# One encoder layer on one core: where the expert weights live, and in which order the first expert pairs, the router and the last rows are worked on

## The chip, the core and the metric

The kernel runs on one core of a Trainium2 chip. The metric is device time in microseconds (us) of one execution. Five engines work side by side, each through its own list of instructions: TensorE (PE, with its weight loads as PEld), VectorE (DVE), ScalarE (ACT), GpSimd (POOL) and SyncE (SP). SyncE issues every large DMA of this kernel, in one order, and waits on semaphores between them.

## The reference, cut to what matters

Input x is (1, 256, 1024) float32. One layer is computed:

```
proj  = x @ w_in                                  # 1024 -> 6144
conv  = pointwise(swish(LN(depthwise31(GLU(proj)))))
attn  = windowed attention (8 heads, band 128) @ w_attn
mixed = (sigmoid gate * conv + sigmoid gate * attn) @ w_out
x1    = LN(alpha * x + mixed; ln1)
top group of 4, then top 2 of its 8 experts per token, with weights
moe   = sum over 32 experts of weight * (silu(x1 @ gate_e) * (x1 @ up_e)) @ down_e
out   = LN(alpha * x1 + moe; ln2)
```

Each token goes to 2 of 32 experts. An expert's gate and up weights are 1024 x 512 floats, 2.10 MB; its down weights are 256 x 1024 floats, 1.05 MB.

## The kernel before, in words

**Projection stages (0 to 233 us).** The dense products run over 72 weight blocks (48 of w_in, 8 each of attention, convolution and output projection). SyncE loads block b into one of four `raw` buffers once GpSimd has split block b-4. ScalarE casts a block to a high part (L611), GpSimd computes the low part (L540), TensorE multiplies with three products (L1334 to L1336). Between the blocks SyncE already loads some expert weights.

**Homes of expert weights.** `slots` has four places, each for one expert's gate/up and down weights. `extra`, `spare` and `late` hold one expert's gate/up weights each. A home of gate/up weights has two halves with a semaphore each. Experts 0, 1 and 4 and the down weights of 0 and 1 are loaded among the blocks of w_in. Slots 2 and 3 lie over `over`, a region that holds the convolution and attention arrays (`h_pad`, `acc`, `qT`, `v_sb`, `prob`, `dist`), so experts 2 and 3 are loaded after the last block has been issued. Expert 5 goes to `spare` once the output projection is done. From expert 6 on there are seven gate/up homes in rotation and four down homes; down weights of pair p are loaded when pair p-2's down products are done (`down_done` of 2(p-1) in SyncE's loop), and gate/up weights run a few experts ahead (`refilled_to`).

**Residual and router (233 to 242 us).** ScalarE copies the four banks of the residual sum to `xt` (`copy_r`). TensorE transposes them (`turn_r`) into banks 0, 1, 2 and again 0; ScalarE copies the parts of token tile 0 and VectorE those of tile 1 to `x1T`. VectorE gathers the moments (`moments`), ScalarE the deviation. ScalarE normalizes from the banks (`normalize_rows`) and casts. TensorE computes logits (L1504, L1512), VectorE picks the experts, TensorE the ranks (L1534 to L1539).

**Pairs.** Experts are worked on two at a time, 64 token places each: 16 pairs. For a pair p: GpSimd copies its tokens from the sorted `xgT` (L569); TensorE makes gate/up products into bank 0 (`gate_up`, L1592); ScalarE applies silu (`swish`, L787); VectorE multiplies with up and weight (`gate_times_up`, L1219); TensorE turns h (`turn_h`, L1616); ScalarE copies it (`copy_hT`, L793); TensorE makes the down products into banks 1 and 2 (`down`, L1627); ScalarE casts y's high part (`split_y_hi`, L800), VectorE subtracts (`split_y_lo`, L1233); TensorE scatters high and low part into banks 3 to 6 (`scatter`, L1642 and L1643). A look-up (`slot_info`, L1576) gives the token and weight of each place; `copy_info` (L776, L779) copies it. VectorE builds the matrices of scatter and look-up (L1226, L1189, L1194). TensorE's order for pair p is: gate/up of p, scatter of p-1 (first half), turn of p, scatter of p-1 (second half), look-up of p+1, down of p.

**First pairs.** Tokens of pairs 0 and 1 are gathered by a product of their own (`gather_first`, L1550 and L1552). Pair 0 runs first. All tokens are then sorted by `gather_sorted` (L1566, L1567) behind the gate/up products of pair 1, through banks 3 to 6, and copied to `xgT`, which lies in `gates` (L806, L1240). GpSimd meanwhile applies gain and offset of the first LayerNorm to `xt` (L558, L561).

**Tail.** After the last scatter VectorE takes the moments of four half rows (L1087), ScalarE the deviation (L726). Half (0,0) is scaled by ScalarE (L852) and finished by GpSimd (L592, L594); the other three by VectorE with two instructions each (L1306, L1307). SyncE stores each half.

## Time and profile before

| what | us |
|---|---|
| median of 3 runs | 475.8 (475.67 to 477.68) |
| the profiled execution's own time | 475.59 |
| its span in the profile | 473.8 |
| TensorE busy | 458.0 (97%) |
| VectorE, ScalarE, GpSimd busy | 248.9, 206.7, 223.1 |
| moved by DMA | 145.13 MB, mean 306 GB/s |

A busy share is a mean over stages with different limits. The slices of the page give it by time; the chain of waits names for each moment the instruction that the end of the span hangs on; a timeline gives the instructions of an engine in order. In a chain of waits "issue" is time in which an engine waited for nothing that the profile shows. Each native float32 product counts as two records of TensorE.

### The profile page before, as it was taken

How to read it: one execution, taken by the hardware profiler on the slowest of the kernel's cores; microseconds unless marked ns; L12 is line 12 of the kernel's file. 1: busy time of each engine (PE TensorE's matmuls, PEld its weight loads, DVE VectorE, ACT ScalarE, POOL GpSimd, SP SyncE). 2: the span in 40 equal slices, each digit the busy share in tenths (PEclk: the TensorE clock that was granted, in tenths of full speed). 3: DMA queues.
4: the chain of work that ended last, by engine and by line, in shares of the span. 5: the costliest groups of instructions: out<-in, count | busy, mean ns of one | idle time of the engine just before them, and what ended most of it. 6: DMA issues, size and time to landing. Idle time of an engine off the chain costs nothing.

```text
span 473.8 us, 7652 instructions
## 1 busy us (share of the span) xinstructions
PE 458.0 (97%) x2776; PEld 321.6 (68%) x2776; DVE 248.9 (53%) x547; ACT 206.7 (44%) x463; POOL 223.1 (47%) x190
## 2 busy tenths in 40 slices
PE   8999999999999999999988999999999999999991
PEld 7999999889999999998863644444444334444430
DVE  3089999869998565466387332222222122222116
ACT  4544455478885678445683232221121122222212
POOL 3998989946956679999448021111111001111002
PEclk9999999999999999999999999999999999999996
DMA  8899989534433444556998999999999999999912
GB/s 282 297 377 361 362 293 356 200 117 144 158 130 121 135 139 174 189 176 245 428 380 326 422 396 423 423 422 419 422 419 422 420 423 420 421 420 423 420 55 91
DMA packets 27091, 145.13 MB, mean 306 GB/s; under 512 B 3120, under 2 KB 3376, under 8 KB 14512
## 3 DMA queue, kind: packets, MB, share of 16 engines
q1 hardware_dynamic: 27056, 144.65, 77.7%
q8 instruction: 23, 0.38, 0.3%
q14 instruction: 12, 0.10, 0.1%
HBM read 143.59 MB, written 1.05 MB: 305 GB/s over the span
## 4 chain that ended last, share of the span: by engine, by line
PE 94%; DVE 3%; ACT 2%; issue 1%; POOL 0%; DVEq 0%; ACTq 0%; POOLq 0%
PE bank L1592 23%; PE bank L1334 14%; PE bank L1336 13%; PE bank L1335 13%; PE bank L1627 12%; PE bank L1642 4%; PE bank L1643 3%; PE bank L1414 1%; PE bank L1392 1%; PE bank L1362 1%; PE bank L1616 1%; PE bank L1566 1%; PE bank L1567 1%; PE bank L1402 1%; PE bank L1421 1%
## 5 line engine op out<-in xcount | busy, mean ns | idle before, releaser
L540 POOL TENSOR_TENSOR w_lo<-raw,w_hi 128x512 fp32r<-128x512 f32 x140 | 182.8, 1323 | 43.8 <-ACT w_hi L611 40.2
L611 ACT CAST w_hi<-raw 128x512 fp32r<-128x512 f32 x140 | 85.4, 620 | 76.7 <-PE bank L1336 73.8
L1334 PE MATMUL bank<-x_hi,w_hi 128*128 128x256 f32 x400 | 115.5, 289 | 0.0
L1336 PE MATMUL bank<-x_hi,w_lo 128*128 128x256 f32 x400 | 113.4, 283 | 0.0
L1335 PE MATMUL bank<-x_lo,w_hi 128*128 128x256 f32 x400 | 113.3, 283 | 0.0
L883 DVE SCALAR_TENSOR_TENSOR bank<-slots,par,bank 128x256 f32<-128x256 f32 x232 | 92.4, 484 | 0.3
L569 POOL COPY raw<-gates 128x512 f32 x28 | 19.8, 708 | 151.1 <-PE bank L1592 134.6
L1592 PE MATMUL bank<-slots,raw 128*64 128x512 f32 x320 | 84.5, 593 | 0.0
L1334 PEld LDWEIGHTS bank<-x_hi,w_hi 128*128 128x128 f32 x400 | 76.8, 192 | 0.6 <-POOL w_lo L540 0.2
L1335 PEld LDWEIGHTS bank<-x_lo,w_hi 128*128 128x128 f32 x400 | 76.8, 192 | 0.3
L1336 PEld LDWEIGHTS bank<-x_hi,w_lo 128*128 128x128 f32 x400 | 76.8, 192 | 0.0
L1627 PE MATMUL bank<-slots,kT 128*64 128x512 f32 x256 | 58.5, 599 | 0.4 <-ACT kT L793 0.4
L1592 PEld LDWEIGHTS bank<-slots,raw 128*64 128x64 f32 x320 | 27.6, 137 | 44.6 <-issue 44.6
L1219 DVE SCALAR_TENSOR_TENSOR pT<-pT,kT,bank 128x256 f32<-128x256 f32 x16 | 7.7, 481 | 91.5 <-ACT pT L787 91.5
L1233 DVE TENSOR_TENSOR w_lo<-bank,w_hi 128x512 fp32r<-128x512 f32 x32 | 22.0, 690 | 56.9 <-ACT w_hi L800 56.9
L787 ACT ACTIVATE pT<-bank 128x256 f32<-128x256 f32 x16 | 6.2, 385 | 97.0 <-PE bank L1592 97.0
L1627 PEld LDWEIGHTS bank<-slots,kT 128*64 128x64 f32 x256 | 17.2, 137 | 28.3 <-issue 28.1
L800 ACT CAST w_hi<-bank 128x512 fp32r<-128x512 f32 x32 | 18.7, 585 | 36.8 <-PE bank L1627 36.8
L1642 PE MATMUL bank<-w_hi,w_lo 128*128 128x512 f32 x64 | 28.3, 441 | 1.2 <-DVE gates L1240 0.9
L1592 PE MATMUL bank<-spare,raw 128*64 128x512 f32 x64 | 28.1, 593 | 0.0
L1592 PE MATMUL bank<-extra,raw 128*64 128x512 f32 x64 | 28.1, 593 | 0.0
L1592 PE MATMUL bank<-late,raw 128*64 128x512 f32 x64 | 28.1, 593 | 0.0
(224 smaller groups left out, 648.8 us busy)
## 6 DMA issues: line engine op xcount, KB each, us to landing
slots<-in_w_gate_up SPq DMA_DIRECT2D x40, 1024.0 KB, 13.3
slots<-in_w_down SPq DMA_DIRECT2D x32, 1024.0 KB, 13.2
raw<-in_w_in SPq DMA_DIRECT2D x45, 512.0 KB, 3.7
extra<-in_w_gate_up SPq DMA_DIRECT2D x8, 1024.0 KB, 12.5
spare<-in_w_gate_up SPq DMA_DIRECT2D x8, 1024.0 KB, 16.4
late<-in_w_gate_up SPq DMA_DIRECT2D x8, 1024.0 KB, 15.8
raw<-in_w_attn SPq DMA_DIRECT2D x8, 512.0 KB, 3.3
raw<-in_w_conv SPq DMA_DIRECT2D x8, 512.0 KB, 3.3
```

Of the source, the lines that this page charges most:

```text
L540: nc.gpsimd.tensor_tensor(w_lo[:, n % SPLIT, m], raw[:, raw_of(b), m], w_hi[:, n % SPLIT, m].bitcast(F32), ALU.subtract).then_inc(w_lo_don ...
L569: ins = nc.gpsimd.tensor_copy(xg[u][:, :, j * WIN:(j + 1) * WIN], xgT[:, :, bass.ds(at, WIN)])
L611: nc.scalar.copy(w_hi[:, n % SPLIT, m], raw[:, raw_of(b), m]).then_inc(w_hi_done, 1)
L800: nc.scalar.copy(y_hi[:, c * HALF:(c + 1) * HALF], y_bank[c][:]).then_inc(y_hi_done, 1)
L883: ins = nc.vector.scalar_tensor_tensor(dst, h_pad[:, i, tap:tap + SEQ], w, so_far, ALU.mult, ALU.add)
L1233: nc.vector.tensor_tensor(y_lo[:, n], y_bank[c][:], y_hi[:, n].bitcast(F32), ALU.subtract).then_inc(y_lo_done, 1)
L1334: mm(dst, ah, bh, start=first, stop=False, **kw)
L1335: mm(dst, ah, bl, start=False, stop=False, **kw)
L1336: return mm(dst, al, bh, start=False, stop=last, **kw)
L1592: ins = mm(gu_bank[j * WIN:(j + 1) * WIN, :], xg[u][:, k, j * WIN:(j + 1) * WIN], weights(j, k // (KT // 2), k % (KT // 2) == 0)[:, n], st ...
L1627: ins = mm(y_bank[c][j * WIN:(j + 1) * WIN, :], hT[:, k, j * WIN:(j + 1) * WIN], w[:, k, c * HALF:(c + 1) * HALF], start=(k == 0), stop=(k ...
L1642: mm(dst, s, y_hi[:, n], start=False, stop=False, skip_group_check=True)
```

## The change

Five edits, made together:

1. **Homes.** Gate/up weights have three homes for pairs (slots 0 and 1; slots 2 and 3; `extra` and `spare`), in rotation. Down weights have a ring of three pairs too (two halves of `late`; slots 0 and 1; slots 2 and 3), and pair 0's lie in `gates`. Pair p is refilled when pair p-3 has read its weights.
2. **Loads.** Experts 2 and 3 and the down weights 4 and 5 are issued between the blocks 61 to 71, as soon as `over` is free; down weights 0 and 1 after the last block; ln1's rows go to `raw`, ln2's rows to slot 2 near the end.
3. **Order of the first pairs** on TensorE: gate/up 0, look-ups 0 and 1, gate/up 1 (into bank 6, with h of pair 0 turned in its middle), down 0, turn 1, `gather_sorted`, look-up 2, down 1, both halves of scatter 0, then pair 2. ScalarE and VectorE follow; their loops over pairs are written out.
4. **Router.** The fourth transpose goes to bank 3; ScalarE copies three of four parts; VectorE copies its part ahead of the last moments; rows are normalized from `xt`; seven products instead of three keep TensorE busy.
5. **Tail.** The second half of the last scatter uses y in float32 (`y_last`) instead of a high and a low part. Token tile 1 is finished as ((r - mean) * gain + std * offset) / std: VectorE the first part, TensorE adds std * offset by a product with a diagonal matrix, ScalarE scales.

```diff
-WARM_START, WARM_ROUTE, WARM_PLACE = 3, 3, 1
+WARM_START, WARM_ROUTE, WARM_PLACE = 3, 7, 1
+RING = 3
+def gu_home_of(e):
+    return (e % 2, 2 + e % 2, EXTRA + e % 2)[e // 2 % RING]
+def wd_home_of(e):
+    if e < 2:
+        return FIRST + e
+    return (LATE + e % 2, e % 2, 2 + e % 2)[e // 2 % RING]
...
@@ SyncE
                 if b == 18:
-                    load_down(0)
-                    load_down(1)
+                    load_down(2)
+                    load_down(3)
...
+                if b == OVER_FREE:                       # OVER_FREE = 61
+                    sp.wait_ge(silu_done, KT)
+                    sp.wait_ge(c_lo_done, KT)
+                    sp.wait_ge(pv_done, HEADS)
+                if OVER_FREE <= b < OVER_FREE + 8 and (b - OVER_FREE) % 2 == 0:
+                    load_half(2 + (b - OVER_FREE) // 4, (b - OVER_FREE) // 2 % 2)
+                if b == OVER_FREE + 8 or b == OVER_FREE + 10:
+                    load_down(4 + (b - OVER_FREE - 8) // 2)
             sp.wait_ge(m_lo_done, KT // 2)
+            load_down(0)
+            load_down(1)
+            sp.wait_ge(w_lo_done, 2 * splits_before(N_BLOCKS))
             sp.dma_start(ln_rows, ln1.broadcast_to([P, 2, D])).then_inc(s_ln1, 16)
-            sp.wait_ge(silu_done, KT)
-            sp.wait_ge(pv_done, HEADS)
-            for e in (2, 3):
-                load_gate_up(e)
-            for e in (2, 3):
-                load_down(e)
...
+            def refill(p):
+                for c in range(2):
+                    sp.wait_ge(gu_done if c else gu_half_done, p - RING + 1)
+                    for e in (2 * p, 2 * p + 1):
                         load_half(e, c)
+            def refill_down(p):
+                sp.wait_ge(down_done, 2 * (p - RING + 1))
+                for e in (2 * p, 2 * p + 1):
                     load_down(e)
+            refill(RING)
+            refill(RING + 1)
+            sp.wait_ge(gathered, KT)
+            refill_down(RING)
+            refill_down(RING + 1)
+            for p in range(RING + 2, PAIRS):
+                refill(p)
+                refill_down(p)
+            sp.wait_ge(gu_done, PAIRS - 2)
+            sp.dma_start(ln2_rows, ln2.broadcast_to([P, 2, D])).then_inc(s_ln2, 16)
...
@@ ScalarE
-            copy_rT(0, 0)
+            copy_rT(0, 0, 0)
             deviation(0)
+            copy_rT(2, 0, 1)
+            copy_rT(3, 1, 1)
             deviation(1)
-            copy_rT(2, 1)
...
+            swish(0)
             copy_info(0, 0)
+            act.wait_ge(info_copied, 1)
+            copy_info(1, 1)
+            copy_hT(0)
+            swish(1)
+            split_y_hi(0)
+            copy_hT(1)
+            copy_sorted()
+            copy_info(2, 0)
+            split_y_hi(1)
+            for p in range(2, PAIRS):
+                pair(p, p % 2)
...
             deviation(0, TT)
+            deviation(1, TT)
+            act.wait_ge(ln_std, 2 * TT)
+            nc.scalar.mul(std_diagonal, ident, mv[:, 1, 2:3]).then_inc(std_turned, 1)
             act.wait_ge(last_shift, 1)
             nc.scalar.activation(xt[:, 0, 0:HALF], out_bank[0][:], ACT.Identity, scale=mv[:, 0, 3:4],
                                  bias=mv[:, 0, 4:5]).then_inc(last_z, 1)
-            deviation(1, TT)
+            for c in range(2):
+                act.wait_ge(offset_added, c + 1)
+                nc.scalar.mul(xt[:, 1, c * HALF:(c + 1) * HALF], out_bank[2 + c][:],
+                              mv[:, 1, 3:4]).then_inc(result_by_act, 1)
...
@@ VectorE
+            for p in range(2):
+                gate_times_up(p, p)
+                build_scatter(p, p)
+                build_gather(p + 2, p)
+            split_y_lo(0)
+            copy_sorted()
+            split_y_lo(1)
...
             inverse(0, TT)
             shift(0, last_shift)
-            last_normal(0, 1)
             inverse(1, TT)
-            last_normal(1, 0)
-            last_normal(1, 1)
+            for c in range(2):
+                r = out_bank[2 + c][:]
+                nc.vector.scalar_tensor_tensor(r, r, mv[:, 1, 0:1], ln2_rows[:, 0, c * HALF:(c + 1) * HALF],
+                                               ALU.subtract, ALU.mult).then_inc(centred_rows, 1)
+            # then half (0, 1), its two instructions as before
...
@@ TensorE
             gather_first()
+            gate_up(0, 0)
             slot_info(0, 0)
-            gate_up(0, 0)
-            for p in range(PAIRS):
+            pe.wait_ge(compact_built, 1)
+            slot_info(1, 1)
+            gate_up(1, 1)                    # turns h of pair 0 after its first half
+            down_pair(0)
+            turn_h(1)
+            gather_sorted()
+            slot_info(2, 0)
+            down_pair(1)
+            pe.wait_ge(xgT_odd, KT // 2)
+            pe.wait_ge(xgT_even, KT // 2)
+            for c in range(2):
+                scatter(0, 0, c)
+            for p in range(2, PAIRS):
                 pair(p)
...
+            for c in range(2):
+                pe.wait_ge(centred_rows, c + 1)
+                mm(out_bank[2 + c][:], std_diagonal, ln2_rows[:, 1, c * HALF:(c + 1) * HALF], start=False, stop=True,
+                   skip_group_check=True).then_inc(offset_added, 1)
```

## Rows read from the trace of the kernel before

**Rows 1.** the page's slices (40 of equal length) and its row of the block splits

```profile
GB/s 282 297 377 361 362 293 356 200 117 144 158 130 121 135 139 174 189 176 245 428 380 326 422 396 423 423 422 419 422 419 422 420 423 420 421 420 423 420 55 91
...
L540 POOL TENSOR_TENSOR w_lo<-raw,w_hi 128x512 fp32r<-128x512 f32 x140 | 182.8, 1323 | 43.8 <-ACT w_hi L611 40.2
```

**Rows 2.** chain of waits, 0 to 464 us; columns: start, length (us), what ran

```profile
246.36 7.04 PE bank L1592 x32
...
255.42 3.66 PE bank L1627 x16
...
259.08 6.87 PE bank L1592 x32
...
273.49 0.82 DVE gates L1240
...
274.35 0.50 PE bank L1642
...
280.40 6.87 PE bank L1592 x32
...
288.39 0.31 PE bank L1616 x2
...
448.62 6.87 PE bank L1592 x32
```

**Rows 3.** timeline of TensorE, look-up; columns: start, length (us), engine, line, operation

```profile
276.54 0.28 PE L1576 MATMUL bank<-info,gat 128*128 128x6 f32 x2
```

**Rows 4.** timelines of ScalarE and TensorE in the router

```profile
235.66 0.78 ACT L742 ACTIVATE xt<-bank,mv 128x512 f32<-128x512 f32 x1
...
240.91 0.27 PE L1534 MATMUL bank<-onehot,sums 128*128 128x64 f32 x1 [1.79 <-DVE onehot L1154]
```

**Rows 5.** timelines of VectorE and GpSimd around the first pairs

```profile
255.67 2.57 DVE L1189 TENSOR_TENSOR gat<-con,rt 128x256 fp32r<-128x256 f32 x1
...
258.16 2.38 DVE L1194 CAST info<-weights 128x4 fp32r<-128x4 f32 x2
...
255.56 4.89 POOL L561 TENSOR_TENSOR xt<-xt,gates 128x1024 f32<-128x1024 f32 x2
...
275.61 2.87 POOL L569 COPY raw<-gates 128x512 f32 x4 [14.57 <-issue]
```

**Rows 6.** timeline of SyncE's queue, DMA issues

```profile
176.46 20.69 SPq L444 DMA_DIRECT2D raw<-in_w_conv  x8
...
220.95 2.74 SPq L419 DMA_DIRECT2D slots<-in_w_gate_up  x4
```

**Rows 7.** windows; columns: busy us of PE, PEld, DVE, ACT, POOL, clock, DMA share, GB/s

```profile
210.00:220.00 10.00, 10.00 (x51) 8.43 (x50) 7.95 (x11) 5.18 (x9) 9.84 (x9) 1.00 0.58 196
...
246.40:250.00 3.60, 3.60 (x18) 1.24 (x20) 3.39 (x13) 3.57 (x7) 0.00 (x0) 1.00 0.40 162
...
452.00:454.00 2.00, 2.00 (x12) 0.60 (x10) 0.00 (x0) 0.00 (x0) 0.00 (x0) 1.00 0.11 45
```

**Rows 8.** DMA issues of 199 to 221 us: count, KB each, median us to landing

```profile
raw<-in_w_out SPq DMA_DIRECT2D x8, 512.0 KB, 4.2
```

**Rows 9.** block casts on ScalarE (L611), 30 to 70 us: idle before them

```profile
  DMA raw<-in_w_in: 2.5, 2
```

**Rows 10.** timelines of ScalarE and GpSimd in the tail

```profile
461.49 0.59 ACT L800 CAST w_hi<-bank 128x512 fp32r<-128x512 f32 x1 [1.13 <-PE bank L1627]
...
467.43 1.26 POOL L592 TENSOR_TENSOR xt<-xt,raw 128x512 f32<-128x512 f32 x1 [35.46 <-ACT xt L852]
```

**Rows 11.** chain of waits, ends of the span

```profile
5.57 6.91 PE bank L1362 x32
...
463.24 1.91 DVE stat L1087 x3
...
470.27 0.75 DVE xt L1307
```

**Rows 12.** window in the tail, columns as in rows 7

```profile
466.00:467.00 1.00, 0.00 (x0) 0.00 (x0) 0.96 (x4) 0.50 (x1) 0.00 (x0) 0.50 0.00 0
```

More of the change, by code:

```diff
@@ L811, in copy_sorted, with pair @@
                         nc.scalar.mul(out_bank[k % 4][:], xt[:, k % 4 // 2, 0:HALF], ALPHA).then_inc(sums_by_act, 1)
[L813 removed]
+            def pair(p, u):
                 swish(p)
[L815 to L816 removed]
                 copy_hT(p)
[L818 removed]
+                if p < PAIRS - 1:
                     copy_info(p + 1, 1 - u)
@@ L1229, in split_y_lo @@
             def split_y_lo(p):
-                for c in range(2):
+                for c in range(1 if is_pair(p, PAIRS - 1) else 2):
                     n = slice(c * HALF, (c + 1) * HALF)
@@ L1286, in _ @@
             for p in range(2):
-                pair(p, p)
-            with dve.Fori(1, PAIRS // 2 - 1) as i:
-                for u in range(2):
-                    pair(i * 2 + u, u)
-            for p in range(PAIRS - 2, PAIRS):
-                pair(p, p % 2, build=False)
-            load = dve.value_load(load_i[0:1, 0:1], min_val=0, max_val=SEQ)
+                gate_times_up(p, p)
[5 more added lines that the diff above has]
+            for p in range(2, PAIRS):
+                if p == PAIRS - 1:
+                    load = dve.value_load(load_i[0:1, 0:1], min_val=0, max_val=SEQ)
+                pair(p, p % 2)
             with dve.If(load > WIN):
@@ L1636, in scatter @@
                     pe.wait_ge(sums_by_dve if c else sums_by_act, TT)
-                pe.wait_ge(y_lo_done, 2 * p + (c + 1))
+                whole = is_pair(p, PAIRS - 1) and c == 1
+                if whole:
+                    pe.wait_ge(y_hi_done, 2 * PAIRS)
+                else:
+                    pe.wait_ge(y_lo_done, 2 * p + (c + 1 - unsplit(p)))
                 for t in range(TT):
@@ L1641, in scatter @@
                     n = slice(c * HALF, (c + 1) * HALF)
+                    if whole:
+                        ins = mm(dst, s.bitcast(F32), y_last, start=False, stop=True, skip_group_check=True)
+                        ins.then_inc(scattered if t == TT - 1 else last_done, 1)
+                        continue
                     mm(dst, s, y_hi[:, n], start=False, stop=False, skip_group_check=True)
```

205 lines of the change are left out of this document (95 added, 110 removed).

## The prediction

> **What bounds the kernel now.** I read the page's slices first, then the chain of waits, then the timelines of each engine where the chain leaves TensorE, and last SyncE's queue and the DMA windows. TensorE is busy for 97% of the span, so only three things can move the end: a gap of TensorE closed, work taken out of the tail that follows it, or a new gap opened. In the slices the reader sees something else as well: from slice 20 on DMA moves about 420 GB/s almost without a break [rows 1]. One pair needs two times 2.10 and two times 1.05 MB, 6.29 MB or 14.95 us at 420.7 GB/s (the middle of those slices), while TensorE needs a pair every 12.94 us: the gate/up products begin at 280.40 for pair 2 and at 448.62 for pair 15, thirteen periods [rows 2]. So loads lose 2.0 us to TensorE with each pair and live on their lead. In the window from 452 on only 45 GB/s are left [rows 7]: the stream ends near 452. Its last piece are two down loads (2.1 MB, 5.0 us), so the last gate/up half lands near 447, and pair 15 begins at 448.62. The lead at the end is a mere 2 us for the first half. An earlier TensorE alone would have run into the loads.
>
> The chain leaves TensorE at three places that the change touches. Gate/up of pair 0 ends at 253.40 and its down products start at 255.42; of these 2.02 us the turn takes 0.31 and the look-up about 0.2 (the 0.28 of its row overlaps the next product's start at about 276.74), so 1.5 are a wait for silu, multiply and copy [rows 2, 3]. After the sort TensorE waits from 273.49 to 274.35, 0.86 us, for VectorE's copy [rows 2]. And behind the last scatter a chain on VectorE runs from 463.24 to 470.27 + 0.75 = 471.02 [rows 11].
>
> **The first pairs.** Every product of before is in the new order too; what goes are the two waits, 1.5 + 0.86 = 2.4 us. Which waits could take their place? I put the new order on a time line. The look-up no longer stands before gate/up 0, which may start 0.2 us earlier, and costs its 0.2 behind it. Gate/up 0 ends near 253.1, the look-ups 0 and 1 at 253.5. ScalarE does silu (0.39) and then two copies of look-ups (0.8 each, by their rows of before), VectorE multiplies by 255.0; the turn in the middle of gate/up 1 comes at 257.0 and finds it done, 2 us to spare. Gate/up 1 ends at 260.7, down 0 at 264.3. Silu and multiply of pair 1 must be ready by then. Here VectorE is slow: beside GpSimd's LayerNorm operations its builds take 2.57 and 2.38 us [rows 5], and they stand ahead of the multiply of pair 1. They end with GpSimd's, near 261, so the multiply ends near 261.9, 2.4 us before the turn needs it. The sort runs 264.6 to 272.1, waits for GpSimd's x1 near 261 (its last pair of operations ends at 260.45 now [rows 5], some 0.5 later then). Look-up and down 1 (3.6) now cover VectorE's last copy. Scatter 0 takes 2.0, and gate/up 2 begins at 277.95 instead of 280.40. It needs GpSimd's token copies: before they began 1.3 us after the last copy at 274.30 and pair 2's two of the four take half of 2.87 [rows 5]; on the new line that is 272.9 + 1.3 + 1.4 = 275.6, in time. I take 2.5 us, with 0.5 and 2.8 as ends: the low end is a copy or build on ScalarE or VectorE that comes 2 us late. The period of 12.94 stays: same products, no wait inside it.
>
> **The router.** TensorE's own work up to the logits stays, so the fourth bank and the other division of copies save at most the 0.3 us that the last copy may hold up. Against that, VectorE's moments of tile 1 now stand behind a copy (0.68), so the shift of tile 0 and with it ScalarE's first normalized row move from 235.66 to about 236.1 [rows 4]. Four rounds of 1.33 end then at 240.9 to 241.0, about where TensorE makes the ranks at 240.91 [rows 4], and it waits for them. Cost 0.1 (0.0 to 0.4). The four extra products (256 columns in float32, 0.43 each: 6.91 us for 16 [rows 11]) lie in its 1.79 us of idle [rows 4] and end at 240.7, just in time; without that cover they would cost up to 1.7.
>
> **Loads.** By the issues of the convolution blocks (8 in 20.69 us, one each 2.9 [rows 6]) block 61 is issued near 190.9. From there six loads of 1.05 MB stand between blocks that leave 42% of DMA time free [rows 7]: 6.3 MB, 15 us of DMA that before began at 220.95 [rows 6]. The region is free by then: VectorE's last low part of the convolution, its last reader, ends at 186.4 in its timeline. On the other side the new homes leave DMA idle from about 239 (expert 5 landed) to 249.8 (first half of gate/up 0 done), where before it idled only in part [rows 7], and again from 270 to 272, as the down loads of pair 3 wait for the sort. From 272.2 on it never stops: 26 down and 22 gate/up loads, 73.4 MB, 174.5 us, end 446.7; the last gate/up half lands 5 us before, at 441.7, and is wanted at 448.62 - 2.5 + 3.4 = 449.5, its first half (436.7) at 446.1. The lead at the end is 8 to 9 us instead of 2. So loads bind nowhere, and the gain of the first pairs reaches the end. ln2's rows follow by 449, wanted at 464.
>
> What the early loads cost the blocks: one now lands 4.2 us after issue [rows 8]. A block's turn on GpSimd comes after three others, 6 x 1.32 = 7.9 us [rows 1], its cast on ScalarE up to 1.5 before that: 6.4 us are allowed. A load ahead of it adds at most 1.05 MB, 2.5 us less what drains before, say 0.9: 5.1. Cost 0; the high end is that of the block casts near 30 us, where whole experts go out at once: 2.5 us in two waits [rows 9], 1.25 for each of six loads, 7.5 us.
>
> **The tail.** Down 15 ends as before; I keep its clock, 461.47. The second scatter half now is two native products of 0.86 (twice the 0.43 for 256 columns [rows 11]) where four of 0.23 stood, but it starts behind the first half at 462.3 and not at 462.85, behind ScalarE's cast (461.49 + 0.59 [rows 10]) alone; TensorE ends at 464.05 in both. What gains is VectorE: without the subtraction the moments begin near 462.0 instead of 463.24 [rows 11] and end near 464.9 instead of 465.94. The shift of tile 0 comes near 465.4, 1.0 earlier, the deviation of tile 1 at 465.5. VectorE then has four instructions of 0.75 instead of six: centred rows at 466.5 and 467.2, half (0,1) at 468.7. GpSimd's two of 1.26 [rows 10] begin at 466.7 and end at 469.3. TensorE adds the offsets at 466.5: 0.86 each at full clock, ScalarE's last scaling ends at 469.1, and with the stores in a row behind GpSimd's the last is issued at 469.8, against 471.05: 1.2 us gained. At half clock each product takes 1.73, the last scaling ends at 470.7 and the gain is 0.3. Now the clock was 0.50 at 466 to 467 [rows 12], TensorE having been idle from 464.05. I take 0.7, between the two, since the moment of the fall need not be the same; the ends are -0.3 (a product waits for both) and 1.3.
> The Trainium skill speaks against this edit: "TensorE: Matmul & The Clock Gate", Part 1 on the clock gate, has TensorE at 1.2 GHz once it was idle and at 2.4 only after sustained work. By that rule, if the fall has come first, the tail gains 0.3; by a clock that still holds, 1.2. The trace agrees that the clock falls after the last scatter.
>
> **The sum.** 2.5 - 0.1 + 0 + 0.7 = 3.1 us off a span of 473.8: 470.7, or 472.5 of the profiled execution's own 475.59 (1.8 lie outside the span). The median of the runs is 0.2 higher, 475.8, and gives 472.7.
>
> **The rivals.**
> 1. *The early loads delay the blocks.* For it: DMA would be 90% full from 191 to 220, GpSimd has no slack there (9.84 of 10 us [rows 7]), so each late block moves the end. Against: the margin of 1.3 us. It decides when a block takes longer than 6.4 us to land. At its full price, 475.8 + 7.5 - 3.1 = 480.2; above 5.5 us of delay the kernel is slower than before by more than 0.5%. Chance 0.07.
> 2. *A new wait takes the place of those removed in the first pairs:* VectorE's builds, slowed by GpSimd, hold the multiply of pair 1, or the copies of the sort hold GpSimd's tokens for pair 2. For it: the long builds of rows 5. Against: margins of 2.4 and 2.3 us. It leaves 0.5 of the 2.5 us: 474.7. Chance 0.15.
> 3. *The change doesn't do what it says in the tail:* TensorE's clock is down and its products, with two more hand-overs, end no earlier than VectorE did alone. For it: rows 12. Gain of the tail 0 to -0.3: 473.4 to 473.7. It is part of my own range at its slow end; chance that it holds alone 0.12 (around the bound of 0.5%).
> 4. *The loads bind,* as the rotation of homes leaves DMA idle for 11 us that I have wrong by some us more, or ScalarE's and VectorE's longer written-out code is fetched late through the full queues. For it: 2 us lost per pair. Against: the lead of 8 us, and TensorE's own code, written out before, which shows no such wait. It would cost 3 to 6 us: 476 to 479. Chance 0.06.
> My forecast, 472.7 with its own range of 471.4 to 473.7, has 0.60.
>
> **How the numbers follow.** A measurement of this kernel tells about 0.5% from no change, 2.4 us: faster means below 473.4. Of my forecast's 0.60, 0.58 is faster; rival 3 adds 0.05 and rival 2 0.01: 0.64. Within 0.5%: 0.02 of mine, 0.07 of rival 3, 0.14 of rival 2 and 0.04 of rivals 1 and 4 (a small price of theirs that eats the gain): 0.27. Slower: the 0.09 that is left of rivals 1 and 4. The range takes in my own terms with their bounds and rival 2: 471.0 (0.4 below the sum of good ends, for what the router may give) to 475.2.
>
> **What would show it.** In the changed profile: gate/up products of pairs 0 and 1 back to back but for two look-ups and a turn; no gap above 0.3 us on TensorE up to gate/up 2, which begins near 278; a period of 12.94 to the end; the early loads' blocks landing in about 5 us and no wait of ScalarE's casts for DMA after 190; DMA silent between about 239 and 250 and done before 450; the first moments of the tail 1.2 us after the last down product's first half was scattered. I am wrong if gate/up 0 begins later than 247, if ScalarE waits for raw blocks, or if gate/up products of a late pair wait for a load. The clock at the two offset products decides the last us.

## The result, and the profile after

The changed kernel takes 473.33 us (median of 5 runs, 473.14 to 473.68), the one before 475.8; the ratio is 0.9942 (95% interval 0.9922 to 0.9962). The profiled execution took 473.26 with a span of 471.5, against 475.59 and 473.8. Forecast were 472.7 and a range of 471.0 to 475.2: the sign and the range hold, and 3.1 us were forecast where 2.3 (spans) to 2.5 (medians) came. The kernel before varies more than this: one of its five runs here took 477.68, and more such runs follow under warm_route.

The slices of the page after (11.8 us each): against [rows 1] GB/s rise in slices 17 to 19 (189 to 224 us), where the early loads now run, and fall in slice 20; slice 21 is a hole.

```profile
GB/s 292 291 378 360 343 301 359 198 120 140 164 133 135 136 134 177 295 358 341 340 187 281 423 325 419 422 423 420 422 420 422 421 422 420 420 420 423 423 116 91
```

The chain of waits after, from the first gate/up products on (start, length in us, what ran):

```profile
246.26 7.02 PE bank L1638 x32
253.28 0.54 PE bank L1622 x4
253.81 3.58 PE bank L1638 x16
257.40 0.37 PE bank L1664 x2
257.77 3.58 PE bank L1638 x16
261.35 3.43 PE bank L1676 x16
264.78 0.37 PE bank L1664 x2
...
272.56 3.58 PE bank L1676 x16
...
278.18 7.02 PE bank L1638 x32
...
446.54 6.87 PE bank L1638 x32
```

These answer to the chain of [rows 2]. The two gaps of before are gone: gate/up 0 ends at 253.28 and gate/up 1 starts at 253.81 behind two look-ups, the turn of pair 0 sits in its middle (257.40), down 0 follows at 261.35 and the sort at 265.15. Pair 2 begins at 278.18 and not at 280.40, pair 15 at 446.54 and not at 448.62. VectorE and GpSimd at the places that the forecast named as risks:

```profile
256.11 2.57 DVE L1233 TENSOR_TENSOR gat<-con,rt 128x256 fp32r<-128x256 f32 x1
258.60 2.40 DVE L1238 CAST info<-weights 128x4 fp32r<-128x4 f32 x2
261.82 0.48 DVE L1263 SCALAR_TENSOR_TENSOR pT<-pT,kT,bank 128x256 f32<-128x256 f32 x1 [0.82 <-ACT pT L824]
```

```profile
274.60 2.88 POOL L605 COPY raw<-gates 128x512 f32 x4 [9.22 <-issue]
```

The builds take 2.57 and 2.40 as in [rows 5]. They end at 261.00, and VectorE then stands idle for 0.82 us until silu of pair 1 is done, so they hold nothing up. The multiply starts at 261.82 and its turn comes at 264.78. GpSimd's copies start at 274.60; pair 2's are done 2.1 us before they are wanted.

DMA after, in windows (busy us of PE, PEld, DVE, ACT, POOL, clock, DMA share, GB/s), beside [rows 7]:

```profile
210.00:220.00 10.00, 10.00 (x51) 8.48 (x50) 7.82 (x12) 5.16 (x9) 9.84 (x8) 1.00 0.96 363
240.00:250.00 10.00, 9.69 (x60) 6.29 (x60) 7.81 (x38) 8.50 (x17) 2.68 (x3) 1.00 0.13 54
270.00:275.00 5.00, 5.00 (x25) 2.98 (x25) 3.01 (x4) 3.12 (x9) 0.40 (x1) 1.00 0.54 190
450.00:454.00 4.00, 4.00 (x19) 1.44 (x16) 0.13 (x1) 0.39 (x1) 0.00 (x0) 1.00 0.33 137
```

The last loads of gate/up weights, in SyncE's queue and by their time to landing (count, KB each, us):

```profile
411.19 9.79 SPq L448 DMA_DIRECT2D slots<-in_w_gate_up  x4
```

```profile
slots<-in_w_gate_up SPq DMA_DIRECT2D x1, 1024.0 KB, 26.4
```

The stream of weights has the forecast hole from 240 and a smaller one at 270, and ends at about 450 + 4 x 137 / 421 = 451.3. The last gate/up half, issued at 420.6, lands at 447.0 (26.4 us later); pair 15 wants it at 450.0. The tail:

```profile
460.07 2.03 DVE L1136 BATCH_NORM_STATS2 stat<-bank 128x6 f32<-128x512 f32 x3 [1.07 <-PE bank L1700]
...
464.67 2.96 PE L1761 MATMUL bank<-slots,sig 128*128 128x512 f32 x4 [2.45 <-DVE bank L1364]
...
465.96 0.69 ACT L902 ACTIVATE xt<-bank,mv 128x512 f32<-128x512 f32 x1 [1.33 <-PE bank L1761]
...
466.67 2.04 SPq L548 DMA_DIRECT2D out_x<-xt  x4
467.66 0.69 ACT L902 ACTIVATE xt<-bank,mv 128x512 f32<-128x512 f32 x1 [1.02 <-PE bank L1761]
```

```profile
464.00:465.00 1.00, 0.33 (x1) 0.30 (x2) 1.00 (x2) 0.63 (x1) 0.22 (x1) 1.00 0.00 0
465.00:466.00 1.00, 1.00 (x3) 0.47 (x2) 0.96 (x3) 0.04 (x1) 1.00 (x1) 0.74 0.00 0
466.00:467.00 1.00, 1.00 (x2) 0.05 (x1) 0.63 (x1) 0.65 (x1) 0.92 (x2) 0.50 0.00 0
```

TensorE's clock falls at about 465.5 (0.74 is the mean of 465 to 466), within the first of the two offset products. TensorE had been idle from 462.2 to 464.67. The second product, the last two of the four records, runs wholly at the low clock.

The start of an execution varies: gate/up 0 began between 246.13 and 247.07 us in profiled executions of kernels that are the same up to there (the changed kernel, old_tail, old_rows, warm_tail, warm_stores). The earliest and the latest of all kernels, homes_swap and then warm_tail, with TensorE's first native products and ScalarE's first residual copy:

```profile
5.09 7.07 PE L1394 MATMUL bank<-gates 128*128 128x256 f32 x32
...
230.74 2.63 ACT L754 COPY xt<-bank 128x512 f32<-128x512 f32 x4 [1.26 <-PE bank L1368]
```

```profile
5.74 7.66 PE L1407 MATMUL bank<-gates 128*128 128x256 f32 x32
...
231.98 2.63 ACT L767 COPY xt<-bank 128x512 f32<-128x512 f32 x4 [1.26 <-PE bank L1381]
```

The products end at 12.16 and 13.40, 1.24 us apart, and the copies are 1.24 apart too: the whole difference arises in the first 13 us. What varies is how fast TensorE runs at first. Its opening products, small ones that only keep it busy, have weight loads of 0.34 us and later of 0.19 us. The tail of the changed kernel has the same two lengths, 0.34 at a granted clock of 0.50 and 0.19 at 1.00:

```profile
465.71 0.34 PEld L1761 LDWEIGHTS bank<-slots,sig 128*128 128x128 f32 x1 [0.29 <-issue]
```

In homes_swap the short ones begin before the products above, in warm_tail only within them, between 6.6 and 7.0 us. By these lengths TensorE starts at the low level and rises sooner or later; the clock row itself reads 1.00 there, so it can't confirm this. In thirteen of the fourteen profiled executions of the table below it takes 218.56 to 218.59 us from the end of these products to the residual copy. The changed kernel's took 218.89. It had lost 0.3 us by 98 us; before that one of ScalarE's casts waited 3.1 us for its block, where no other execution has a wait above 2.5. The early loads come later than that, and six of the thirteen have them: they cost the projection stages nothing.

So I compare stages, from the profiled execution of each kernel. "Residual copy" is the start of ScalarE's first copy of the residual sum, "gate/up 0 to 2" goes from the start of pair 0's gate/up products to the start of pair 2's, "cast" is the start of ScalarE's copy of the last half of y, "first moments" are VectorE's first in the tail. All in us:

| kernel | median | residual copy to gate/up 0 | gate/up 0 to 2 | gate/up 2 to 15 | cast to first moments | cast to last result | cast to end of span |
|---|---|---|---|---|---|---|---|
| before | 475.8 | 15.32 | 34.04 | 168.22 | 1.75 | 9.53 | 12.31 |
| changed | 473.33 | 15.08 | 31.92 | 168.36 | 0.66 | 8.94 | 12.09 |
| late_loads | 473.29 | 15.09 | 31.92 | 168.37 | 0.66 | 7.99 | 11.94 |
| old_order | 476.59 | 15.20 | 34.02 | 168.22 | 0.66 | 9.64 | 12.82 |
| old_homes | 478.77 | 15.08 | 31.93 | 173.02 | 0.64 | 9.21 | 12.34 |
| homes_swap | 473.35 | 15.08 | 31.92 | 168.51 | 0.65 | 8.87 | 11.99 |
| old_router | 473.45 | 15.19 | 31.93 | 168.36 | 0.64 | 7.96 | 11.89 |
| hoist_only | 475.58 | 15.33 | 34.02 | 168.22 | 1.22 | 8.99 | 11.81 |
| old_tail | 473.25 | 15.08 | 31.93 | 168.37 | 1.22 | 8.99 | 11.60 |
| old_rows | 472.47 | 15.08 | 31.93 | 168.35 | 0.66 | 8.62 | 11.28 |
| warm_tail | 473.92 | 15.09 | 31.92 | 168.37 | 0.66 | 8.00 | 11.87 |
| warm_stores | 473.37 | 15.08 | 31.92 | 168.37 | 0.66 | 8.00 | 11.97 |
| simple | 473.34 | 15.08 | 31.92 | 168.37 | 0.67 | 8.63 | 11.48 |
| warm_route | 476.08 | 15.31 | 34.04 | 168.21 | 1.76 | 9.53 | 12.39 |

From gate/up 15 to the cast it is 12.87 everywhere. The columns repeat to within 0.03 where two kernels have the same code there, so a stage tells 0.1 us where a median does not tell 0.5. The last two columns are excepted, since the clock and the stores come in: the end of the span differs by 0.2 between kernels with the same tail (hoist_only and old_tail, old_rows and simple). The change's 2.3 us are +0.14 up to the residual copy, then -0.24, -2.12, +0.14 and -0.22 up to the end of the span. Nearly all of it lies between gate/up 0 and 2, where the order of the first pairs was changed.

### The profile page after: what moved, and what is told of

The parts are those of the page before. It is cut to its first block, busy times and chain, and to the rows that moved or that the text cites. A ratio compares the mean times of both kernels' runs of the same rounds, so it can differ in the third digit from the quotient of the medians.

```text
span 471.5 us, 7554 instructions
## 1 busy us (share of the span) xinstructions
PE 463.3 (98%) x2788; PEld 323.0 (69%) x2788; DVE 244.2 (52%) x543; ACT 208.9 (44%) x467; POOL 223.2 (47%) x190
## 4 chain that ended last, share of the span: by engine, by line
PE 94%; ACT 3%; DVE 1%; issue 1%; POOL 0%; ACTq 0%; DVEq 0%; POOLq 0%
PE bank L1638 23%; PE bank L1379 14%; PE bank L1381 13%; PE bank L1380 13%; PE bank L1676 12%; PE bank L1699 4%; PE bank L1700 3%; PE bank L1459 1%; PE bank L1437 1%; PE bank L1407 1%; PE bank L1664 1%; DVE stat L1136 1%; PE bank L1613 1%; PE bank L1612 1%; PE bank L1447 1%
## 5 line engine op out<-in xcount | busy, mean ns | idle before, releaser
L1638 PE MATMUL bank<-slots,raw 128*64 128x512 f32 x352 | 77.7, 593 | 0.0
L1638 PEld LDWEIGHTS bank<-slots,raw 128*64 128x64 f32 x352 | 25.0, 137 | 48.9 <-issue 48.7
L1676 PE MATMUL bank<-slots,kT 128*64 128x512 f32 x160 | 36.5, 598 | 0.0
L1638 PE MATMUL bank<-extra,raw 128*64 128x512 f32 x80 | 35.2, 593 | 0.0
L1638 PE MATMUL bank<-spare,raw 128*64 128x512 f32 x80 | 35.2, 593 | 0.0
L1699 PE MATMUL bank<-w_hi,w_lo 128*128 128x512 f32 x62 | 27.3, 440 | 0.0
L1638 PEld LDWEIGHTS bank<-extra,raw 128*64 128x64 f32 x80 | 10.9, 137 | 22.6 <-issue 22.6
L1700 PE MATMUL bank<-w_lo 128*128 128x512 f32 x62 | 24.5, 396 | 0.0
```

Source lines behind the costliest of these rows:

```text
L1638: ins = mm(gu_bank(p)[j * WIN:(j + 1) * WIN, :], xg[u][:, k, j * WIN:(j + 1) * WIN], weights(j, k // (KT // 2), k % (KT // 2) == 0)[:, n], ...
L1676: ins = mm(y_bank[c][j * WIN:(j + 1) * WIN, :], hT[:, k, j * WIN:(j + 1) * WIN], by_row(weights(j))[:, k, n], start=(k == 0), stop=(k == H ...
L1699: mm(dst, s, y_hi[:, n], start=False, stop=False, skip_group_check=True)
L1700: ins = mm(dst, s, y_lo[:, n], start=False, stop=True, skip_group_check=True)
```

## The experiments

**late_loads: the early loads undone.**

```diff
-                if b == OVER_FREE:
...
-                if OVER_FREE <= b < OVER_FREE + 8 and (b - OVER_FREE) % 2 == 0:
-                    load_half(2 + (b - OVER_FREE) // 4, (b - OVER_FREE) // 2 % 2)
-                if b == OVER_FREE + 8 or b == OVER_FREE + 10:
-                    load_down(4 + (b - OVER_FREE - 8) // 2)
...
+            for e in (2, 3):
+                load_gate_up(e)
...
             load_down(0)
             load_down(1)
+            for e in (4, 5):
+                load_down(e)
```

> The changed kernel with one thing undone: gate/up weights 2 and 3 and down weights 4 and 5 are issued behind the last block (after 220 us) and no longer between blocks 61 and 71. Theory A, the early loads only fill time that is free later: in the changed kernel DMA stands idle from 240 to 249.9 (0.13 busy), and six loads of 2.5 us moved there leave it idle from about 248 only. Then nothing moves: 473.3 us within 0.3, gate/up 2 at 278.2, the stream of weights ends at 451.3 as now, blocks land in 4.2 us again. Theory B, the early loads give the stream its lead: the stream ends 10 us or more later, gate/up products of the last pairs wait for their weights, 476 to 480 us.

473.29 us, ratio to before 0.9931 (0.9909 to 0.9952), and no stage up to the first moments changed. (The last result came 0.95 us earlier since the clock had not fallen in this execution; see the tail below.) Its windows:

```profile
210.00:220.00 10.00, 10.00 (x53) 8.50 (x52) 7.49 (x11) 4.82 (x9) 9.85 (x8) 1.00 0.55 187
240.00:250.00 10.00, 9.69 (x59) 6.43 (x60) 7.75 (x40) 8.51 (x16) 3.01 (x3) 1.00 1.01 417
450.00:454.00 4.00, 4.00 (x19) 1.30 (x16) 0.00 (x0) 0.20 (x1) 0.00 (x0) 1.00 0.47 195
```

The loads fill 240 to 250, where the changed kernel had 54 GB/s, and the stream ends at 450 + 4 x 195 / 421 = 451.9, against 451.3 in the changed kernel; 0.3 of that is its later start. Theory A: the early loads only move the hole.

**old_order: the first pairs in the order of before.**

```diff
-            gate_up(0, 0)
-            slot_info(0, 0)
-            slot_info(1, 1)
-            gate_up(1, 1)
-            down_pair(0)
-            turn_h(1)
-            gather_sorted()
...
+            slot_info(0, 0)
+            gate_up(0, 0)
+            turn_h(0)
+            slot_info(1, 1)
+            down_pair(0)
+            gate_up(1, 1)
+            gather_sorted()
+            scatter(0, 0, 0)
+            turn_h(1)
+            scatter(0, 0, 1)
...
```

> The changed kernel with the order of the first two pairs put back on TensorE, ScalarE and VectorE (turn and down of pair 0 directly behind its gate/up, the sort behind gate/up 1, all gate/up products in bank 0); homes, loads, router and tail stay. Theory A, the order brought the gain up to pair 2: gate/up 2 begins at 280.3 instead of 278.18, the period stays 12.94, 475.4 us. Theory B, homes and loads brought it: gate/up 2 stays near 278.2 and the time at 473.3.

476.59 us, ratio 0.999 (0.9974 to 1.0005). The chain:

```profile
247.07 7.04 PE bank L1636 x32
...
281.09 6.87 PE bank L1636 x32
```

34.02 us from gate/up 0 to 2, as before: the order is worth 2.10 to 2.12 us (theory A). The median lies 1.2 above the expectation. Its 12 runs fall in two groups, four at 474.8 to 475.3 with a mean clock of 0.999 to 1.000, which is what was expected, and eight at 476.4 to 476.9 with 0.995 to 0.996. The profiled execution (476.73) is of the second group. It started 0.8 us later than the changed kernel's, and it took 9.64 us to the last result: both offset products ran at the low clock, four records in 3.65 us where the changed kernel had 2.96. No execution of the first group was profiled.

```profile
467.44 3.65 PE L1757 MATMUL bank<-slots,sig 128*128 128x512 f32 x4 [2.45 <-DVE bank L1363]
```

**old_homes: homes, refills and row places of before under the new order.**

```diff
-EXTRA, GU_HOMES = SLOTS, SLOTS + 2
+SPARE, TOKENS, EXTRA = SLOTS, SLOTS + 1, SLOTS + 2
+HOMES = SLOTS + 3
...
-            refill(RING)
-            refill(RING + 1)
...
+            refill((6, 7))
+            for p in range(SLOTS // 2, PAIRS):
+                sp.wait_ge(down_done, 2 * (p - 1))
+                for e in (2 * p, 2 * p + 1):
+                    load_down(e)
+                if p == SLOTS // 2:
+                    refill((8, 9))
+                refill(range(refilled_to(p - 1), refilled_to(p)))
```

> The changed kernel with the homes, the refills and the places of the LayerNorm rows of before (seven gate/up and four down homes, nothing of experts 2 and 3 before the last block); order of the pairs, router and tail stay changed. Theory A, an earlier TensorE alone runs into the loads: before, the last gate/up halves landed about 446 and 448 where pair 15 began at 448.6; now it begins at 446.5, so TensorE waits up to 1 us in the late pairs: 473.5 to 474.4 us. Theory B, the stream moves with TensorE, as its refills are released by it, and nothing binds: 473.3. Theory C, the gain is that of the homes: 475 or more.

478.77 us, ratio 1.0045 (1.0028 to 1.0062): slower than before, and by far more than theory A had. Theory C's number (475 or more) came, and its reason is refuted by the next run. TensorE waits for down weights of pairs 7 and 8. The rows say "issue", but the second load of each pair, issued at 330.8 and 343.7, lands 22.5 and 24.5 us later, at 353.3 and 368.2, just as the products begin:

```profile
353.39 3.65 PE L1664 MATMUL bank<-slots,kT 128*64 128x512 f32 x16 [0.71 <-issue]
...
368.30 3.65 PE L1664 MATMUL bank<-slots,kT 128*64 128x512 f32 x16 [1.91 <-issue]
```

and once more in pair 14 (1.37 us ahead of its down products and 0.5 inside its gate/up products). SyncE's queue shows where the lead went:

```profile
250.18 4.25 SPq L442 DMA_DIRECT2D slots<-in_w_gate_up  x4
265.12 0.81 SPq L451 DMA_DIRECT2D slots<-in_w_down  x2
265.97 2.21 SPq L442 DMA_DIRECT2D slots<-in_w_gate_up  x4
```

```profile
260.00:270.00 10.00, 10.00 (x47) 5.62 (x44) 5.52 (x11) 3.39 (x6) 1.72 (x2) 1.00 0.55 214
```

In the new order down 0 comes behind gate/up 1, and SyncE stands at the wait for it until 265.1, while slots 2 and 3 were free from 257 and 261 on: 55% busy, 4.5 us of DMA lost where the stream has none to spare. The waits add up to 4.65 us (173.02 against 168.37).

**homes_swap: the same with that refill ahead of the wait.**

```diff
             refill((6, 7))
+            refill((8, 9))
             for p in range(SLOTS // 2, PAIRS):
                 sp.wait_ge(down_done, 2 * (p - 1))
                 for e in (2 * p, 2 * p + 1):
                     load_down(e)
-                if p == SLOTS // 2:
-                    refill((8, 9))
```

> The kernel with the changed order and the homes of before (478.8 us, 4.7 us of waits of TensorE for weights at pairs 7, 8 and 15), with SyncE's refills of experts 8 and 9 put ahead of its wait for the first down products. Theory A, what bound there was DMA idle from 260 to 265, since SyncE stood at that wait while slots 2 and 3 were free already: the stream gets 4.5 us back, the waits shrink to 0 to 0.6 us, 473.6 to 474.2 us. Theory B, seven and four homes are too few for the new order whatever the order of refills: the waits at pairs 7 and 8 stay and the time is 477 or more.

473.35 us, ratio 0.9935 (0.9912 to 0.9959).

```profile
260.00:270.00 10.00, 10.00 (x48) 5.97 (x45) 4.79 (x11) 4.07 (x7) 0.98 (x2) 1.00 1.02 428
```

Moving one refill in SyncE's list gives back 4.5 us between gate/up 2 and 15 (173.02 to 168.51). The medians differ by 5.4; in the profiled executions 0.7 of that is an earlier start and 0.35 the end. Theory A, with less left over than it had: 0.14 us of waits. The kernel with the homes of before is as fast as the changed one (473.33). Seven and four homes were enough; what the new order needed was this refill released by what frees it.

**old_tail, hoist_only, old_rows: the tail taken apart.** old_tail undoes both edits of the tail; hoist_only is the kernel before with the read of the load register ahead of the last pair, a line that I had not costed; old_rows keeps the float32 scatter and undoes the offset on TensorE.

```diff
# hoist_only, against the kernel before (VectorE)
             for p in range(PAIRS - 2, PAIRS):
+                if p == PAIRS - 1:
+                    load = dve.value_load(load_i[0:1, 0:1], min_val=0, max_val=SEQ)
                 pair(p, p % 2, build=False)
-            load = dve.value_load(load_i[0:1, 0:1], min_val=0, max_val=SEQ)
# old_rows, against the changed kernel (VectorE)
+            last_normal(0, 1)
             inverse(1, TT)
-            for c in range(2):
...
+            last_normal(1, 0)
+            last_normal(1, 1)
# old_tail: the same, and (ScalarE, TensorE; VectorE's loop goes with it)
-                    whole = is_pair(p, PAIRS - 1) and c == 1
+                    whole = False
```

> The changed kernel with the whole tail of before (last scatter in high and low part, token tile 1 finished by VectorE, order of stores). Theory A: the new tail is worth what the trace shows from the end of the last down product to the last result, 9.55 us before and 8.99 now, less 0.3 us of slower last stores: 473.6 to 473.9 us. Theory B, the offset product at a falling clock gives all of it back: 473.3 or less. In the trace: last down product ends at 459.4 as in the changed kernel, the last result comes 9.5 us later.

> The kernel before with one line moved: VectorE reads the load register ahead of the last pair and not behind it. Theory A, this alone is what the tail of the change gained: the first moments begin 1.3 us after the last down product instead of 1.8, and the time falls by 0.5 to 475.3 to 475.5 us. Theory B, the read costs nothing and the earlier moments came from the missing subtraction: 475.8 to 476.0 as the kernel before.

> The changed kernel with the float32 product of the last scatter kept and token tile 1 finished by VectorE as before, stores in the order of before. Theory A, the float32 scatter gives 0.35 us (moments begin 0.71 instead of 1.27 after the last down product, tile 1's variance comes at 3.65 instead of 4.0), and the offset on TensorE gives nothing, as four stores then fall together: last result 8.7 us after the last down product, end of the span 11.3 after it (12.14 in the changed kernel, 11.65 with the whole tail of before), 472.5 to 472.9 us. Theory B, the scatter's two long products hold the moments of tile 1 by as much as the missing subtraction gives: 11.65, 472.8 to 473.3.

old_tail: 473.25 us, ratio 0.9928 (0.9906 to 0.9949). The number is theory B's, the picture is neither's: I expected the last result 9.5 us after the last down product, but it comes as early after the cast as in the changed kernel (8.99 against 8.94), and the span ends 0.5 us earlier. hoist_only: 475.58, ratio 0.9995 (0.9976 to 1.0014). The gain is too small for the median (5 of its 12 runs lie at 476.9 to 477.6), but the stage is clear, and theory A's. Its first moments (the cast is at 461.89):

```profile
463.11 1.88 DVE L1087 BATCH_NORM_STATS2 stat<-bank 128x6 f32<-128x512 f32 x3
```

against 463.24 in [rows 11] for a cast at 461.49. 1.22 us and not 1.75 behind the cast, and the end 0.5 earlier: the read of a register between the last pair and the moments cost 0.5 us. old_rows: 472.47, ratio 0.9914 (0.9889 to 0.9939), the fastest of all, as theory A had it. Its first moments and its last result:

```profile
459.98 2.03 DVE L1130 BATCH_NORM_STATS2 stat<-bank 128x6 f32<-128x512 f32 x3 [1.07 <-PE bank L1696]
...
467.19 0.75 DVE L1359 SCALAR_TENSOR_TENSOR xt<-bank,mv,slots 128x512 f32<-128x512 f32 x1
```

So the tail splits like this, from the cast to the end of the span: moving the register read gains 0.50 (12.31 to 11.81; the same tail in the changed kernel's surroundings, old_tail, has 11.60). The float32 scatter gains another 0.32 (11.60 to 11.28). The offset on TensorE takes back 0.81 (to 12.09). Each of these ends may be off by the 0.2 by which equal tails differ; the last results repeat better, and there the scatter gains 0.36 (8.99 to 8.62 and 8.63).

**warm_tail, warm_stores: the offset products at full clock.**

```diff
+            keep_warm(turn_bank[:, 0:SEQ], 5, iota[:, 0:SEQ])
             pe.wait_ge(s_ln2, 16)
             pe.wait_ge(std_turned, 1)
# warm_stores, in addition (SyncE)
-            sp.wait_ge(result_by_pool, 1)
-            store(0, 0)
             sp.wait_ge(result_by_act, 2)
             store(1, 1)
+            sp.wait_ge(result_by_pool, 1)
+            store(0, 0)
```

> The changed kernel with five products more (256 columns, float32, into the free bank of the turns) between the last scatter and the two offset products, so that TensorE does not stand idle from 462.2 to 464.7. Theory A, the falling clock costs the tail its gain: the four records of the offset products take 0.21 each instead of up to 0.43, ScalarE's last scaling ends at 467.3 instead of 468.35, GpSimd's half at 467.4 is last, the last store is issued near 467.9 instead of 468.4: 472.8 us against 473.3. Theory B, the stores behind GpSimd's half or the hand-overs between engines set the end anyway: 473.3, with the products at full clock.

> As the kernel with five products more, and the store of half (1,1) waited for before that of half (0,0). Theory A: both halves are ready at 467.3 and 467.4 and one store issue takes 0.4, so the order moves the end by at most 0.1: 472.7 to 472.9 us. Theory B, a half kept waiting behind GpSimd's costs its full 0.4: 472.4.

```profile
465.49 1.96 PE L1762 MATMUL bank<-slots,sig 128*128 128x512 f32 x4 [0.29 <-DVE bank L1364]
...
467.34 1.80 SPq L548 DMA_DIRECT2D out_x<-xt  x4
```

```profile
466.00:467.00 1.00, 1.00 (x4) 0.38 (x2) 0.96 (x3) 0.38 (x1) 0.92 (x2) 1.00 0.00 0
```

The clock stays at 1.00, the four records take 1.96 instead of 2.96 us, and the last result comes 0.94 us earlier after the cast. The end gains only 0.2 (11.87 in warm_tail and 11.97 in warm_stores, against 12.09). The times are 473.92 us (ratio 0.9938, 0.9915 to 0.9962) and 473.37 (0.9932, 0.9909 to 0.9955); warm_tail's profiled execution started 0.8 us later than the changed kernel's. Theory B: the stores set the end. All four are issued within 1.8 us, and from the last result to the end of the span it takes 3.9 us here, 3.15 in the changed kernel and 2.6 to 2.8 where VectorE gives the halves one after the other (old_tail, before). In which order two of them go does not matter: that is the picture of warm_stores' theory A, but its time (472.7 to 472.9) did not come.

**simple: everything of before but the order of pairs, the router, the refill, the register read and the float32 scatter.** It is homes_swap with the tail of old_rows.

> Homes, places of rows and loads of before with the refills of experts 8 and 9 put ahead, the changed order of the first pairs, the changed router, the float32 last scatter, rows of tile 1 finished by VectorE as before. Theory A, order and tail carry the whole gain and homes and early loads none once that one wait of SyncE is out of the way: same as the kernel with the changed homes and this tail, 472.5 to 473.0. Theory B, the changed homes keep a lead that this kernel lacks: TensorE waits for weights in late pairs, 474 or more.

473.34 us, ratio 0.9926 (0.9899 to 0.9954), runs from 472.18 to 474.46. Theory A by the stages, each as in old_rows (the end 11.48 against 11.28). The median misses its range (472.5 to 473.0) and lies 0.9 above old_rows. The profiled executions are 0.9 apart too, 0.7 of it in the start (gate/up 0 at 246.86 against 246.16) and 0.2 in the end; the spread of the six runs does not let me say more.

**old_router.** The router's five edits undone together (bank 0 for the fourth transpose, VectorE's two copies, rows from the banks, 3 products for 7).

> The changed kernel with the router of before (fourth transpose in bank 0, VectorE copies two parts, rows normalized from the banks, three products to keep TensorE busy). Theory A, the reordering is worth nothing: from the first residual copy to gate/up 0 it takes 15.1 us in the changed kernel and 15.3 in the one before, which has a look-up of 0.2 in it; 15.1 again, 473.3 us. Theory B, the four extra products or the moved copy matter: 14.8 or 15.5, and without the extra products the clock falls ahead of the first gathers, which would add some us.

473.45 us, ratio 0.993 (0.9908 to 0.9953); 15.19 against 15.08, between the theories: the new router gains 0.11 us where I had booked a loss of 0.1. TensorE's rank products in the changed kernel and in old_router:

```profile
240.91 0.30 PE L1579 MATMUL bank<-onehot,sums 128*128 128x64 f32 x1 [0.17 <-ACT xt L778]
```

```profile
241.34 0.27 PE L1583 MATMUL bank<-onehot,sums 128*128 128x64 f32 x1 [1.79 <-DVE onehot L1202]
```

They begin 9.73 and 9.88 us after the residual copy. With the new copies the logits end 0.26 us earlier after it. The ranks then wait for ScalarE's normalized rows, as the forecast had it, and that takes a part back. Of old_router's 8 runs one lies 1.7 us above the rest.

**warm_route: the kernel before with seven products behind the logits.**

```diff
-WARM_START, WARM_ROUTE, WARM_PLACE = 3, 3, 1
+WARM_START, WARM_ROUTE, WARM_PLACE = 3, 7, 1
```

> The kernel before with one number changed: seven products instead of three behind the logits, to keep TensorE busy while VectorE picks the experts. The 33 runs of the kernel before so far fall in two groups, 475.2 to 476.1 us (17 runs) and 477.1 to 478.1 (16 runs), the second with a mean clock of 0.988 to 0.992 where the first has 0.991 to 0.995; of the changed kernel's 5 none lies 1 us above the others, of the one with the router of before 1 of 8 does. Theory A, in the second group TensorE's clock falls in the 1.8 us of idle before the ranks, and the four products prevent it: all runs between 475.0 and 476.3, median 475.6. Theory B, the groups come from elsewhere (the waits of the first pairs, or the start): a third to a half of the runs above 477 again.

476.08 us, ratio 0.9989 (0.9975 to 1.0004), 12 runs from 475.31 to 476.80, none in the upper group. The kernel before ran 67 times beside all these experiments, 31 of them at 477.1 to 478.1 (mean clock mostly 0.988) and 36 at 475.2 to 476.4 (0.991 to 0.995); that is also why its median lay between 476.05 and 477.44 beside the different experiments. If each run had a chance of 31/67 of falling above, independently of the others, twelve below would come about once in 1,700 cases. So the times and the mean clock (0.991 to 0.995) speak for theory A, with two reservations. Three of the twelve runs, at 476.5 to 476.8, lie above the lower group, and the median is 0.5 above the 475.6 that the theory had. And no execution of the upper group was profiled: that the clock falls in this gap was not seen. In the profiled execution the four products change nothing (15.31 us from the residual copy to gate/up 0, against 15.32).

## Why the prediction was right, and where it was not

**First pairs: right, in the mechanism and in the size.** Forecast 2.5, less 0.1 for the router; measured from the residual copy to gate/up 2 are 2.36. Both waits of [rows 2] are gone and none took their place. Gate/up 0 began at 246.26, as forecast (with some luck, since the start was 0.14 later), gate/up 2 at 278.18 against 277.95: look-ups and turns take 0.1 more than I gave them. Rival 2 did not come: the multiply of pair 1 was ready 2.5 us early (2.4 forecast), the tokens of pair 2 2.1 (2.3 forecast). In one link the forecast was wrong without harm: the multiply waited for silu and not for the builds. old_order shows that taking the order back takes the gain back, simple that the order brings it with the homes of before.

**The period: 0.14 missed.** The gate/up products of pair 2 now follow a scatter and take 7.02 us; behind down products they take 6.87. In the rows a scatter product stands as 128*128, gate/up and down as 128*64. I had counted the products and not the change between the two kinds.

**The router: -0.1 forecast, +0.1 measured.** The wait for the normalized rows came; what I put at nothing was the earlier end of the logits (0.26). Beside it there is something that I did not see: the four extra products, costed at nothing and worth nothing in a profiled execution, seem to take away the upper group of times.

**Loads: right that nothing binds, wrong on what keeps it so.** I gave the early loads and the homes the credit for a lead of 8 to 9 us. The lead of the last half was 3 us. The stream ended at 451.3, 2 us later than worked out: it resumed at about 273.9 (66 GB/s from 273 to 274, 303 from 274 to 275) where I had 272.2. And the last gate/up half, with three loads (7.5 us) behind it, landed 3 us later than its place in the stream says; I can't say why. And late_loads and homes_swap run as fast without either. That an earlier TensorE "alone would have run into the loads" came true in old_homes by 4.65 us, but not by the mechanism stated, the shift of 2 us. It was SyncE's list, in which a refill stood behind a wait that the new order delays. Blocks behind early loads landed in 4.4 to 5.9 us (5.1 forecast) and no cast after 188 us waited for one: rival 1 did not come.

**The tail: the term that was mis-sized.** Forecast 0.7, measured 0.22. Two mistakes nearly cancelled in the last result (0.59 earlier) and not in the end. I left out the register read that the diff moves (0.50 gained). The first moments came 1.09 us earlier after the cast, near the 1.24 that I gave to the missing subtraction, but 0.53 of it is the register read: that this number nearly held was luck. For the offset I took the mean of two clocks and priced only the products and the issuing of the stores, not that four stores which fall together end later. As measured the edit loses at either clock: 0.6 at the high one, 0.8 in the profiled execution and 1.5 when both products ran slow (old_rows against warm_tail, the changed kernel and old_order). At the high clock the last result comes earlier (8.00 against 8.62), but the four halves come together and their stores end later; where the clock falls, the last result comes later as well. Rival 3, to which I gave 0.12, was right on this edit where the clock fell (8.94 or 9.64 against 8.62). Where the clock held its reason fails, and the stores alone take the gain back. The rule of the Trainium skill that I set against this edit ("TensorE: Matmul & The Clock Gate", Part 1) agrees with the changed kernel, where the clock falls behind TensorE's idle spell, and with warm_tail, where products fill the spell and it stays at 1.00. But in late_loads and old_router it had not fallen by the end of the products, with the same idle spell ahead, so it is a matter of the execution.

**A version that beats the kernel before, and probably the changed one,** is old_rows: 472.47 us, 0.9914 (0.9889 to 0.9939), with a span of 470.6, 3.2 us under that of before. Against the changed kernel it is 0.9 by the medians and 0.8 by the last stage, but simple, with the same tail, had a median of 473.34.

## What to carry to other kernels

When products are reordered, walk through the DMA queue's list of waits again: a refill behind a wait that the new order delays cost 4.5 us here, and new buffers were not the cure. Cost an edit of a tail to the end of the last store and not to the last result, and look for reads of a value into a register on the engine that the tail waits for. Compare stages of profiled executions rather than medians when an edit is worth less than the spread of the start.

## What the runs showed of the hardware that I had not expected

- Up to the first gate/up products nearly the same code took 245.8 to 247.1 us, and the whole difference arises in the first 13 us: the first native products began between 5.09 and 5.74 and ran 7.07 to 7.66 us, with weight loads of 0.34 us before and 0.19 after some moment that differs from execution to execution.
- Four stores of 256 KB issued within 2 us landed in 2.4 to 2.5 us each (medians), spread over 3.4 us in 2.1.
- An idle gap of TensorE of 1.8 us behind the logits goes with a second group of times 2 us above the first; none of 12 runs fell into that group once four more products filled the gap. The profiled executions show a clock of 1.00 there either way.
